# A 32-row block form of the chunk inverses in a two-layer decoder's recurrence, with an earlier state load and a new step order

## The chip, the cores and the metric

The kernel runs on one core of a Trainium2 chip. The metric is the device time of one launch in microseconds (us). The time before is the median of three runs.

## What is computed

One inference step of a two-layer decoder for 256 prompt tokens and 8 samples of 8 tokens (320 tokens, width 2048). Layer A mixes tokens with the RWKV-7 recurrence over 32 heads of size 64; layer B is stick-breaking attention over a paged cache of 2048 keys per sample. The change touches the recurrence alone:

```python
def step(S, inp):
    r_t, w_t, k_t, v_t, kk_t, a_t = inp
    sa = jnp.einsum("bhvk,bhk->bhv", S, -kk_t)
    S = (S * w_t[:, :, None, :] + sa[..., None] * (kk_t * a_t)[:, :, None, :]
         + v_t[..., None] * k_t[:, :, None, :])
    o_t = jnp.einsum("bhvk,bhk->bhv", S, r_t)
    return S, o_t
```

## The kernel before, in words

The program has three parts in a row: the projections r, k, v, g of layer A; the recurrence; and a trunk with the output projection, layer B's projections and the attention. TensorE runs the projections as three passes (high and low parts) over 320 tokens.

The recurrence treats 16 tiles of 128 channels, two heads each, one head in partitions 0 to 63 and one in 64 to 127 (`halves`). The 256 prompt tokens are four chunks of 64 (NCH = 4), and the 64 sample tokens are a fifth (CH = 5). Inside a chunk the recurrence is a triangular system: its strictly triangular 64x64 matrix has to be inverted. The samples' chunk has 8x8 blocks only. Each tile passes three stages, one slot apart:

- **F** (front) makes decays and the scaled rows AR, BZ and KZ.
- **P** (products) makes the chunk matrices, and from them the inverse X. AB (L1517) and s4 (L1523) multiply BZ and KZ with AR; D keeps the 8x8 diagonal blocks. Their inverse Y comes by doubling: D transposed (Dt), D squared (D2, D2t), its fourth power (D4t), W and Y. The rest of the triangle follows the same way: Yt, E, Et, E2, E2t, E4t, Z1, Z2, X. Each of these fifteen steps is the helper `each` (L1495 to L1499): one 64x64 by 64x64 matmul for each chunk and half, ten where all five chunks take part and eight where four do. A transpose is such a matmul with the identity I2. Vn, Bn and Kn are transposes too and stay. ScalarE or VectorE takes every result out of PSUM (L1220, L1378).
- **R** (run) walks through the chunks: U, SA, S, ST for each of four, and U4, SA4, O4, SN, Q4 for the samples. Q4 (L1618) multiplies the samples' loaded states s0t; SN (L1649) multiplies 32-row pieces. Then O0 to O3, mean, cen, csq, var, lnv, rstd, on, ong, oy, y, xh and xl normalise the outputs and split them for the next projection. SA0 takes the X of its tile.

In slot n, F works on tile n, P on tile n - 1 and R on tile n - 2; there are 18 slots. The order in which each engine issues the steps of a slot is written out in ORDER (L328 to L337): a step such as R.t.SA0 is stage, engine (t TensorE, v VectorE, a ScalarE, g GpSimd) and name. `side_by_side` merges the three stages by their place in it. All engines are in order; between them the steps wait on semaphores through `Marks`. PSUM banks go round in TensorE's order of steps, four for P and three for R (`Banks`). Slot 0 also runs the last group of projection g, slot 17 most of the first group of wo.

SyncE loads the inputs of the tiles. Within a slot it waits for the steps that free s, k, r, a and v (the last is freed by TensorE's Vn), loads them, and then loads the samples' states s0t of tile n - 1 (L1071 to L1076).

Of the kernel before, what the change touches and what calls it, by code (L numbers as in the profile page):

```python
# [18 lines left out]
ALU = mybir.AluOpType  # L19
# [10 lines left out]
L = 64  # L30
NCH = SEQ // L
# [297 lines left out]
F.a.sq F.a.ka1 R.t.U0 R.a.Q4 R.a.SA4 R.t.Q4 R.a.O0 P.t.AB R.t.SA0 R.g.Vnx R.v.U0 F.v.cs R.t.U4 P.t.s4 R.t.S0  # L329
F.a.kk0 R.v.SA0 R.t.SA4 R.a.SP1 R.t.O0 R.a.O4 F.t.ss R.t.U1 R.v.U4 P.a.Dt R.t.O4 P.t.Dt R.t.SA1 P.v.D R.t.SN  # L330
F.a.Pc P.a.D2t R.a.SP2 R.v.ST0 P.v.D4s P.a.D2 P.a.D4t R.t.S1 P.t.D2t P.t.D2 R.g.SAx F.a.ln F.g.k2 R.t.U2
R.a.O2 P.v.FR R.a.O1 F.a.rn F.a.Pi P.t.W R.t.SA2 R.a.O3 R.v.U1 P.v.KK F.a.Pm R.v.SA1 P.t.D4t R.t.S2 R.t.O2
P.v.s3 R.v.SNa R.v.ST1 F.g.csm R.v.U2 F.v.ssm R.a.SP3 R.v.SA2 P.g.ID P.a.Yt P.a.Vn R.t.O1 R.a.csq P.v.W
P.a.Et P.a.E R.t.U3 R.v.ST2 R.v.U3 P.t.Y R.t.SA3 P.t.Vn R.t.O3 R.a.lnv R.a.rstd P.t.Yt R.t.mean P.a.E2t
F.t.bon P.t.Et P.t.E R.v.SA3 P.v.Y R.t.var F.g.Rz F.g.ka P.t.Z1 P.a.E2 P.t.E2t F.v.rk R.v.cen F.v.kk P.t.E2
F.v.Az R.a.ong P.a.Bn P.a.E4t R.a.xh P.t.Bn F.v.Bz F.v.bonus P.v.Z1 P.t.Z2 P.t.E4t R.v.on P.v.Z2 P.t.Kn
R.t.S3 R.v.ST3 P.a.Kn F.g.Kz P.v.X P.t.X R.g.SNb R.g.oy R.g.y R.v.xl""".split()  # L337
# [50 lines left out]
def products_of_chunk(c_, pe, q, m, k, half=None, banks=None):  # L388
# [11 lines left out]
READ_BY = {"AB": ("v", "D", "FR", "KK"), "s4": ("v", "D4s", "s3"), "Vn": ("a", "Vn"), "Bn": ("a", "Bn"),  # L400
# [50 lines left out]
def make_masks(c_, pool):

    masks, blk, blkm, I2, m8, mFI, mSI, m3, keep, mJ = (
        c_.masks, c_.blk, c_.blkm, c_.I2, c_.m8, c_.mFI, c_.mSI, c_.m3, c_.keep, c_.mJ)
# [31 lines left out]
    for m in (m8, mFI, mSI, m3):  # L486
# [9 lines left out]
    made(pool.tensor_copy(mFI[:, 1], mSI[:, 1]))  # L496
    made(pool.tensor_tensor(mFI[:, 0], mSI[:, 0], m8[:], ALU.subtract))
# [455 lines left out]
def recurrence(nc, c_, a):  # L953

    with ExitStack() as ctx:
# [19 lines left out]
        D, Dt, D2, D2t, D4t, W = (sb(x, [P, CH, L]) for x in ("D", "Dt", "D2", "D2t", "D4t", "W"))  # L975
        Yt, E, Et = (sb(x, [P, NCH, L]) for x in ("Yt", "E", "Et"))
        FR, KK = ([sb(f"{x}{j}", [P, NCH, 2, L]) for j in range(2)] for x in ("FR", "KK"))
        S3 = [sb(f"S3{j}", [P, 3, L]) for j in range(2)]
        Y, X, Vn, Bn, Kn = ([sb(f"{x}{j}", [P, CH, L]) for j in range(2)] for x in ("Y", "X", "Vn", "Bn", "Kn"))
# [13 lines left out]
        gate_exp, gate_ln = sem("gate_exp"), sem("gate_ln")  # L993
        g_stored = 16 * 16 + 1
# [24 lines left out]
        def _(sp):  # L1019
# [25 lines left out]
            for slot in range(TILES + 2):  # L1045
# [120 lines left out]
        def _(act):  # L1166
# [1683 lines left out]
```

## Time and profile before

| | us |
|---|---|
| median of 3 runs | 2034.37 (2025.7 to 2036.75) |
| profiled execution, its own time | 2030.11 |
| its span | 2028.4 |
| TensorE matmuls busy in the span | 1886.5 (93%) |
| VectorE, ScalarE, GpSimd busy | 1014.0, 815.6, 244.3 |
| slots 2 to 16 of the recurrence | 338.0, from 540.2 to 878.2 |

The window that begins at 522.9 us is slot 1 from its AB on, the one at 540.2 us slots 2 to 16, the one at 810.0 us one slot of these. A slot is taken from the first matmul of Q4 to the next tile's. In the trace each fp32 matmul leaves two records, so a step of ten matmuls shows as x20. A record's duration is from its start to its modelled end, and records overlap: how long a step holds TensorE is read from its start to the start of what follows. VectorE, ScalarE and GpSimd instructions likewise overlap a little. "issue" is time for which the profile shows nothing that was waited for.

### The profile page before, as it was taken

What the parts mean: (1) busy time and instruction counts of PE and PEld (TensorE: products, weight loads), DVE (VectorE), ACT (ScalarE), POOL (GpSimd) and SP (SyncE); (2) the same over time, 40 slices, a digit from 0 to 9 for tenths busy, and PEclk for the clock granted to TensorE, in tenths of its full rate; (3) what the DMA queues carried; (4) which work ended last, traced back from release to release, by engine and by line L of the source; (5) the groups of instructions that cost most, each with busy time, mean ns of one, the idle gap of its engine ahead of it and who ended that gap; (6) DMA issues with size and microseconds to landing.
All of it is one profiled execution on the core that took longest, in us unless ns stands there. A gap on an engine that the chain in (4) does not pass through costs nothing.

```text
span 2028.4 us, 49604 instructions
## 1 busy us (share of the span) xinstructions
PE 1886.5 (93%) x20798; PEld 1623.7 (80%) x20798; DVE 1014.0 (50%) x1686; ACT 815.6 (40%) x1443; POOL 244.3 (12%) x308
## 2 busy tenths in 40 slices
PE   7999999999999999999999899999999999777797
PEld 7988999999888888879998677677777677343697
DVE  7744363634455556634544543443455444677344
ACT  4234232334455555523333333332333444655233
POOL 0200000000244444413200000000000000110032
PEclk9999999999999999989999999999999999999899
DMA  7545555544132322105488999999999999999541
GB/s 284 173 143 177 165 181 171 170 158 149 56 106 85 91 89 84 55 22 189 150 333 315 411 414 419 397 425 424 425 424 424 407 422 383 415 407 378 230 145 73
DMA packets 122959, 505.55 MB, mean 249 GB/s; under 512 B 16033, under 2 KB 55330, under 8 KB 77474
## 3 DMA queue, kind: packets, MB, share of 16 engines
q1 hardware_dynamic: 122754, 502.60, 64.9%
q8 instruction: 155, 2.54, 0.5%
q14 instruction: 50, 0.41, 0.1%
HBM read 470.24 MB, written 32.32 MB: 248 GB/s over the span
## 4 chain that ended last, share of the span: by engine, by line
PE 31%; DMA 16%; DVE 3%; ACT 2%; issue 2%; SPq 1%; DVEq 0%; ACTq 0%
DMA at_vraw<-in_cache_v 16%; PE psP L2566 8%; PE psP L2568 7%; PE psP L2567 7%; PE at_psO L2616 5%; PE at_psS L2595 3%; SPq L1979 1%; PE psP L2661 0%; PE at_psT L2607 0%; DVE wlo L2328 0%; SPq L2019 0%; DVE at_o_new L2483 0%; ACT at_p_w L2286 0%; ACT at_p_w L2284 0%; SPq L1997 0%
## 5 line engine op out<-in xcount | busy, mean ns | idle before, releaser
L2566 PE MATMUL psP<-xhi,whi 128*128 128x320 f32 x1488 | 477.6, 321 | 2.5 <-DVE xlo L2453 1.9
L2567 PE MATMUL psP<-xlo,whi 128*128 128x320 f32 x1488 | 462.3, 311 | 0.0
L2568 PE MATMUL psP<-xhi,wlo 128*128 128x320 f32 x1488 | 462.2, 311 | 0.0
L2566 PEld LDWEIGHTS psP<-xhi,whi 128*128 128x128 f32 x1488 | 282.0, 189 | 67.1 <-issue 66.4
L2328 DVE TENSOR_TENSOR wlo<-wraw,whi 128x2048 fp32r<-128x2048 f32 x92 | 212.9, 2315 | 209.0 <-ACT whi L2154 208.7
L2154 ACT ACTIVATE whi<-wraw 128x2048 fp32r<-128x2048 f32 x92 | 176.0, 1913 | 279.9 <-PE psP L2568 278.3
L2567 PEld LDWEIGHTS psP<-xlo,whi 128*128 128x128 f32 x1488 | 282.3, 190 | 0.1
L2568 PEld LDWEIGHTS psP<-xhi,wlo 128*128 128x128 f32 x1488 | 281.8, 189 | 0.0
L131 PE MATMUL psP<-xhi,whi 128*128 128x320 f32 x704 | 218.4, 310 | 2.8 <-DVE wlo L166 2.3
L132 PE MATMUL psP<-xlo,whi 128*128 128x320 f32 x704 | 217.8, 309 | 0.0
L133 PE MATMUL psP<-xhi,wlo 128*128 128x320 f32 x704 | 217.8, 309 | 0.0
L2616 PE MATMUL at_psO<-at_vraw,at_st 128*32 128x512 f32 x1000 | 129.2, 636 | 54.9 <-DMA at_vraw<-in_cache_v 45.8
L166 DVE TENSOR_TENSOR wlo<-wraw,whi 128x2048 fp32r<-128x2048 f32 x47 | 107.8, 2293 | 144.7 <-ACT whi L160 144.7
L160 ACT ACTIVATE whi<-wraw 128x2048 fp32r<-128x2048 f32 x47 | 89.8, 1910 | 161.9 <-PE psP L133 161.9
L131 PEld LDWEIGHTS psP<-xhi,whi 128*128 128x128 f32 x704 | 132.2, 188 | 3.9 <-DVE wlo L166 2.9
L132 PEld LDWEIGHTS psP<-xlo,whi 128*128 128x128 f32 x704 | 132.2, 188 | 0.1
L133 PEld LDWEIGHTS psP<-xhi,wlo 128*128 128x128 f32 x704 | 132.2, 188 | 0.0
L2595 PE MATMUL at_psS<-at_kraw,at_qp 128*32 128x256 f32 x2048 | 124.9, 385 | 0.2 <-DMA at_kraw<-in_cache_k 0.2
L2616 PEld LDWEIGHTS at_psO<-at_vraw,at_st 128*32 128x32 f32 x1000 | 27.5, 112 | 109.0 <-DMA at_vraw<-in_cache_v 59.4
L2231 ACT ACTIVATE at_st<-at_psT 128x256 f32<-128x256 f32 x64 | 24.3, 380 | 203.3 <-PE at_psT L2607 203.3
L2595 PEld LDWEIGHTS at_psS<-at_kraw,at_qp 128*32 128x32 f32 x2048 | 60.9, 111 | 46.3 <-issue 13.2
L394 PE MATMUL psP<-xhi,whi 128*128 128x320 f32 x256 | 89.2, 348 | 1.3 <-DVE wlo L166 0.8
(378 smaller groups left out, 3212.9 us busy)
## 6 DMA issues: line engine op xcount, KB each, us to landing
wraw<-in_weights SPq DMA_DIRECT2D x160, 1024.0 KB, 6.1
at_kraw<-in_cache_k SPq DMA_DIRECT2D x96, 1024.0 KB, 11.1
at_vraw<-in_cache_v SPq DMA_DIRECT2D x94, 1024.0 KB, 11.1
at_kraw<-in_cache_k SPq DMA_DIRECT2D x64, 512.0 KB, 9.5
at_vraw<-in_cache_v SPq DMA_DIRECT2D x62, 512.0 KB, 10.6
rw_s0t<-in_s0T SPq DMA_DIRECT2D x16, 256.0 KB, 3.1
o_wkv_s<-rw_SN SPq DMA_DIRECT2D x16, 256.0 KB, 2.3
resT<-in_xT SPq DMA_DIRECT2D x8, 320.0 KB, 5.1
```

The lines of the kernel that those rows point to most:

```text
L131: pe.matmul(out, wh, c_.xhi[:, kc, :], start=(kc == 0), stop=False)
L132: pe.matmul(out, wh, c_.xlo[:, kc, :], start=False, stop=False)
L133: last = pe.matmul(out, wl, c_.xhi[:, kc, :], start=False, stop=(kc == NM - 1))
L160: act.activation(c_.whi[:, q % 2], c_.wraw[:, q], ACT.Copy).then_inc(c_.whi_ready, 1)
L166: dve.tensor_tensor(c_.wlo[:, q % 2], c_.wraw[:, q], c_.whi[:, q % 2], ALU.subtract).then_inc(c_.wlo_ready, 1)
L2154: act.activation(whi[:, i % 2], wraw[:, q], ACT.Copy).then_inc(c_.whi_ready, 1)
L2328: dve.tensor_tensor(wlo[:, i % 2], wraw[:, q], whi[:, i % 2], ALU.subtract).then_inc(c_.wlo_ready, 1)
L2566: pe.matmul(out, wh, c_.xhi[:, kc, :], start=(kc == 0), stop=False)
L2567: pe.matmul(out, wh, c_.xlo[:, kc, :], start=False, stop=False)
L2568: last = pe.matmul(out, wl, c_.xhi[:, kc, :], start=False, stop=(kc == NM - 1))
L2595: last = pe.matmul(psS[32 * j:32 * j + 32, 0:BK].rearrange("p (t s) -> p t s", t=KB), qp[:, b % 2, j, 32 * i:32 * i + 32], keys, start=(i ...
L2616: last = pe.matmul(psO[32 * g:32 * g + 32, :], st[:, k % 2, pg, 32 * g:32 * g + 32], values_of(k, pg, g), start=(k % NBLK == 0 and pg == 0 ...
```

## The change

The inverses are made for 32x32 diagonal blocks of the 64x64 triangles instead of whole. The buffers D to Y hold such blocks in compact form, [128, 5, 32]: partitions 0 to 31 the first block of head 0, 32 to 63 its second, and so on, so a chunk needs four matmuls of 32x32 by 32x32 (`by_fourths`), one in each quarter of the partitions. AA computes the diagonal blocks from BZ and AR directly (64 rows, 32 stationary columns, 32 moving). The steps D2, W, D4t and Y run over five chunks, E, Z1, E2t and X over four. The transposes Dt, D2t, Yt, Et and X1t are done by VectorE, 32x32 at a time. E2, E4t, Z2 and the transposing or second-copy matmuls Dt, D2t, Yt and Et leave TensorE: inside 32 rows there are four 8x8 blocks, and E to the power four is zero. The off-diagonal 32x32 corner of X follows from the two diagonal inverses and the corner A12 of the product AB, by two steps of eight matmuls each (Ht, XB), of 64 stationary and 32 moving columns. Y4 (GpSimd) spreads the samples' compact blocks into X, and Xa (ScalarE) the first diagonal block. s4 no longer computes the samples' product that AA now gives. FR shrinks to the half that R reads; F (VectorE) masks the part of AA that E needs.

The load of s0t moves to the head of SyncE's slot. ORDER is new. In the last slot the pieces of the wo split hang on rstd and on instead of SP3 and cen. GpSimd makes the additional masks before the recurrence. The waits that free BZ and KZ name the last of their readers.

```diff
--- before.py
+++ after.py
+R.t.Q4 R.t.U0 P.t.AB R.a.Q4 F.a.sq P.t.AA R.v.U0 R.t.U4 P.v.D R.t.SA0 P.t.Kn R.v.U4 P.g.ID R.v.SA0 P.v.KK R.t.S0
+R.g.Vnx R.t.SA4 F.t.ss R.v.ST0 R.a.SA4 P.v.FR F.a.ka1 R.g.SAx R.t.U1 P.v.Dt P.a.A12 R.t.O4 R.v.U1 R.t.SA1 R.a.O4
+P.t.D2 R.v.SA1 F.v.cs R.t.S1 P.a.D2 R.a.SP1 R.t.SN P.v.D2t F.g.csm R.v.ST1 P.v.F R.a.SP2 P.a.Kn R.t.U2 R.v.SNa F.a.Pc
+F.g.k2 P.t.W F.a.kk0 R.v.U2 P.t.D4t P.v.W R.t.SA2 P.a.D4t R.t.O1 R.v.SA2 F.v.ssm R.t.O0 R.a.O1 R.t.S2 F.a.Pm P.t.Y
+R.v.ST2 F.a.ln R.t.U3 R.a.O0 R.a.SP3 P.t.Vn F.a.Pi R.v.U3 P.v.Y F.a.rn R.t.SA3 R.t.O2 R.v.SA3 P.v.Yt R.t.O3 F.v.rk
+R.a.O2 P.t.E R.a.O3 F.v.kk R.t.S3 P.a.E R.t.mean P.a.Vn P.v.Et F.g.ka P.t.E2t R.v.cen P.t.Z1 P.g.Y4 P.a.E2t R.a.csq
+P.t.s4 F.g.Kz P.v.Z1 R.v.ST3 P.t.X R.t.var F.g.Rz P.v.X P.v.s3 F.t.bon P.v.X1t R.a.lnv P.t.Ht R.a.rstd P.t.Bn R.v.on
+P.a.Ht F.v.Bz P.t.XB R.a.ong P.a.Bn F.v.Az R.g.oy P.a.Xa P.a.XB F.v.bonus R.g.y R.g.SNb R.a.xh R.v.xl
...
@@ make_masks @@
-    made(pool.tensor_tensor(mFI[:, 0], mSI[:, 0], m8[:], ALU.subtract))
+    made(pool.memset(c_.side[:], 0.0))
+    for g in range(4):
+        rows, cols = slice(HL * g, HL * g + HL), slice(HL * (g % 2), HL * (g % 2) + HL)
+        made(pool.tensor_copy(c_.mD[rows, :], m8[rows, cols]))
+        made(pool.tensor_copy(c_.mF[rows, :], mSI[rows, 0, cols]))
+        made(pool.tensor_copy(c_.I4[rows, :], c_.ident[rows, rows]))
+        made(pool.memset(c_.side[rows, g % 2:g % 2 + 1], 1.0))
+    made(pool.tensor_tensor(c_.mF[:], c_.mF[:], c_.mD[:], ALU.subtract))
...
@@ recurrence, buffers @@
-        D, Dt, D2, D2t, D4t, W = (sb(x, [P, CH, L]) for x in ("D", "Dt", "D2", "D2t", "D4t", "W"))
-        Yt, E, Et = (sb(x, [P, NCH, L]) for x in ("Yt", "E", "Et"))
+        D, Dt, D2, D2t, D4t, W, Y = (sb(x, [P, CH, HL]) for x in ("D", "Dt", "D2", "D2t", "D4t", "W", "Y"))
+        FI, Yt, E, Et, E2t, Z, XD, XDt = (sb(x, [P, NCH, HL]) for x in ("FI", "Yt", "E", "Et", "E2t", "Z", "XD", "XDt"))
+        A12, Ht = sb("A12", [P, NCH, L]), sb("Ht", [P, NCH, L])
+        FR = [sb(f"FR{j}", [P, NCH, L]) for j in range(2)]
...
@@ sync, at the head of each slot, ahead of the loads of s, k, r, a and v @@
+                if 0 <= t - 1 < TILES:
+
+                    if t >= 3:
+                        R.t.wait(sp, "Q4", t - 3)
+                        R.v.wait(sp, "SNa", t - 3)
+                    sp.dma_start(s0t[(t - 1) % 2][:], a["s0T"][t - 1]).then_inc(s0_in[(t - 1) % 2], 16)
...
@@ gpsimd, products @@
+                    elif name == "Y4":
+                        Q.v.wait(pool, "Y", t)
+                        if t >= 2:
+                            R.t.wait(pool, "SA4", t - 2)
+                        Q.g.done(pool.tensor_tensor(X[t % 2][:, NCH].rearrange("p (i s) -> p i s", i=2),
+                                                    Y[:, NCH].unsqueeze(1).to_broadcast([P, 2, HL]),
+                                                    c_.side[:].unsqueeze(2).to_broadcast([P, 2, HL]), ALU.mult), name)
...
@@ scalar, products @@
+                    if name == "A12":
+                        Q.v.wait(act, "FR", t)
+                        ps = psP[:, banks_p.of("AB")].rearrange("p (c x l) -> p c x l", c=NCH, l=L)[:, :, 0, HL:L]
+                        Q.a.done(act.activation(A12[:, :, HL:L], ps, ACT.Copy, scale=c_.side[:, 0:1]), name)
+                    elif name == "Xa":
+                        Q.v.wait(act, "X", t)
+                        Q.a.done(act.activation(X[t % 2][:, 0:NCH, 0:HL], XD[:], ACT.Copy, scale=c_.side[:, 0:1]), name)
+                    elif name in ("Ht", "XB"):
+                        Q.t.wait(act, name, t)
+                        out = Ht[:, :, 0:HL] if name == "Ht" else X[t % 2][:, 0:NCH, HL:L]
+                        ps = psP[:, banks_p.of(name), 0:NCH * HL].rearrange("p (c l) -> p c l", l=HL)
+                        Q.a.done(act.activation(out, ps, ACT.Copy), name)
...
@@ vector, products @@
+                    elif name == "Dt":
+                        Q.v.wait(dve, "D", t)
+                        Q.v.done(dve.transpose(flat(Dt[:]), flat(D[:])), name)
...
+                        out, base, n = {"W": (W, W, CH), "Y": (Y, W, CH), "Z1": (Z, Y, NCH), "X": (XD, Z, NCH)}[name]
...
@@ tensor, products @@
+                def by_fourths(out, lhs, rhs, n):
 
                     for c in range(n):
+                        for r in fourths:
+                            last = pe.matmul(out[r, c * HL:c * HL + HL], lhs[r, c], rhs[r, c], start=True, stop=True)
+                    return last
+
+                def corner(out, lhs, rhs):
+
+                    for c in range(NCH):
                         for r in halves:
-                            last = pe.matmul(out[r, c * L:c * L + L], lhs[r, c], I2[r, :] if rhs is None else rhs[r, c],
-                                             start=True, stop=True)
+                            last = pe.matmul(out[r, c * HL:c * HL + HL], lhs[r, c], rhs[r, c], start=True, stop=True)
                     return last
...
+                    elif name == "AA":
+                        F.v.wait(pe, "Az", t)
+                        F.v.wait(pe, "Bz", t)
+                        for c in range(CH):
+                            for g, rows in enumerate(fourths):
+                                r, cols = halves[g // 2], slice(HL * (g % 2), HL * (g % 2) + HL)
+                                last = pe.matmul(ps[rows, c * HL:c * HL + HL], BZ[j][r, c, cols], ar[r, c, 0, cols],
+                                                 start=True, stop=True)
...
+                    elif name == "Ht":
+                        Q.a.wait(pe, "A12", t)
+                        Q.v.wait(pe, "X1t", t)
+                        Q.t.done(corner(ps, A12, XDt), name)
+                    elif name == "XB":
+                        Q.a.wait(pe, "Ht", t)
+                        Q.v.wait(pe, "X", t)
+                        Q.t.done(corner(ps, Ht, XD), name)
```

## Rows read from the trace of the kernel before

**Rows 1.** Windows: length; PE, PEld, DVE, ACT, POOL busy (x); clock, DMA share, GB/s.

```profile
522.90:540.20 17.30, 14.60 (x378) 12.95 (x378) 9.10 (x19) 9.11 (x22) 6.21 (x7) 1.00 0.33 103
540.20:878.20 338.00, 320.08 (x8575) 293.39 (x8575) 196.87 (x510) 189.17 (x538) 137.73 (x160) 1.00 0.27 79
810.00:831.00 21.00, 20.77 (x572) 19.25 (x574) 12.67 (x33) 12.14 (x35) 8.34 (x11) 1.00 0.26 76
```

**Rows 2.** Who waited for whom, TensorE, slots 2 to 16: total us, times, longest.

```profile
PE psP L1499 <- issue: 6.0, 8, 1.4
PE rw_psR L1618 <- DMA rw_s0t<-in_s0T: 1.2, 1, 1.2
```

**Rows 3.** Timeline of TensorE in one slot: start, us, instruction group.

```profile
698.11 1.09 PE L1618 MATMUL rw_psR<-rw_AR,rw_s0t 64*64 64x16 f32 x32
699.02 0.45 PE L1517 MATMUL psP<-rw_AR,rw_BZ 64*64 64x128 f32 x4
...
700.80 0.31 PE L1600 MATMUL rw_psR<-rw_U,rw_X 64*64 64x64 f32 x4
...
705.60 0.75 PE L1499 MATMUL psP<-rw_Dt,rw_D 64*64 64x64 f32 x20
706.18 0.75 PE L1499 MATMUL psP<-rw_D,rw_Dt 64*64 64x64 f32 x20
...
713.52 0.66 PE L1499 MATMUL psP<-rw_FR,rw_Yt 64*64 64x64 f32 x16
713.99 0.74 PE L1473 MATMUL rw_psR<-stage_a,rw_blkm 64*64 64x320 f32 x4
714.53 0.66 PE L1499 MATMUL psP<-rw_Y,rw_Et 64*64 64x64 f32 x16
```

**Rows 4.** Timeline of TensorE around SN, the one step of another tile shape.

```profile
704.05 0.31 PE L1600 MATMUL rw_psR<-rw_U,rw_X 64*64 64x64 f32 x4
704.29 0.66 PE L1649 MATMUL rw_psR<-rw_Vnx,rw_Kn 32*64 32x256 f32 x8
704.78 0.61 PE L1649 MATMUL rw_psR<-rw_SAx,rw_Bn 32*64 32x256 f32 x8
705.32 0.33 PE L1600 MATMUL rw_psR<-rw_Vn,rw_Kn 64*64 64x64 f32 x4
705.48 0.28 PE L1600 MATMUL rw_psR<-rw_SA,rw_Bn 64*64 64x64 f32 x4
```

**Rows 5.** Timeline of TensorE in the attention, a step with 32 stationary columns.

```profile
1751.23 0.65 PE L2650 MATMUL psP<-at_kN,at_qn 128*32 128x64 f32 x32
```

**Rows 6.** Groups of TensorE weight loads, whole span: 32 and 64 stationary columns.

```profile
L2595 PEld LDWEIGHTS at_psS<-at_kraw,at_qp 128*32 128x32 f32 x2048 | 60.9, 111 | 46.3 <-issue 13.2 <-DMA at_kraw<-in_cache_k 0.6
L1618 PEld LDWEIGHTS rw_psR<-rw_AR,rw_s0t 64*64 64x64 f32 x512 | 17.0, 135 | 6.4 <-issue 4.6 <-DMA rw_s0t<-in_s0T 1.4 <-ACT xhi L1262 0.4
```

**Rows 7.** Groups of VectorE, slots 2 to 16.

```profile
L1378 DVE TENSOR_TENSOR rw_Y<-psP,rw_W 128x320 f32<-128x320 f32 x15 | 7.2, 481 | 0.0
L1370 DVE TENSOR_TENSOR rw_S<-psP,rw_m 128x192 f32<-128x192 f32 x15 | 5.2, 348 | 0.0
```

**Rows 8.** Timeline of ScalarE, the end of R in the same slot.

```profile
714.76 0.53 ACT L1251 ACTIVATE stage_a<-rw_psR,consts 128x320 f32<-128x320 f32 x1 [0.16 <-PE rw_psR L1473]
...
717.37 0.65 ACT L1258 ACTIVATE stage_a<-stage_a,vec 128x320 f32<-128x320 f32 x1 [0.82 <-DVE stage_a L1415]
...
719.93 0.47 ACT L1262 ACTIVATE xhi<-rw_yv 128x320 fp32r<-128x320 f32 x1 [1.32 <-POOL rw_yv L1161]
```

**Rows 9.** Timeline of VectorE, the end of R in the same slot.

```profile
716.72 0.61 DVE L1415 TENSOR_TENSOR stage_a<-stage_a 128x320 f32<-128x320 f32 x1
...
720.44 0.49 DVE L1418 TENSOR_TENSOR xlo<-rw_yv,xhi 128x320 fp32r<-128x320 f32 x1
720.85 0.22 DVE L1389 COPY rw_U<-rw_psR 128x64 f32<-128x64 f32 x1
```

**Rows 10.** Page, part 2: GB/s in 40 slices of 50.7 us.

```profile
GB/s 284 173 143 177 165 181 171 170 158 149 56 106 85 91 89 84 55 22 189 150 333 315 411 414 419 397 425 424 425 424 424 407 422 383 415 407 378 230 145 73
```

More of the change, by code:

```diff
@@ L328 @@
 ORDER = """
[L329 to L337, printed above, removed]
+R.t.Q4 R.t.U0 P.t.AB R.a.Q4 F.a.sq P.t.AA R.v.U0 R.t.U4 P.v.D R.t.SA0 P.t.Kn R.v.U4 P.g.ID R.v.SA0 P.v.KK R.t.S0
[6 more added lines that the diff above has]
+P.a.Ht F.v.Bz P.t.XB R.a.ong P.a.Bn F.v.Az R.g.oy P.a.Xa P.a.XB F.v.bonus R.g.y R.g.SNb R.a.xh R.v.xl
+""".split()
 AT = {x: k / len(ORDER) for k, x in enumerate(ORDER)}
@@ L1290, in beside @@
                 elif slot == TILES + 1:
-                    for q, step in ((2, "SP3"), (3, "xh")):
+                    for q, step in ((2, "rstd"), (3, "xh")):
                         for k in range(QC):
@@ L1439, in beside @@
                 elif slot == TILES + 1:
-                    for q, step in ((2, "cen"), (3, "xl")):
+                    for q, step in ((2, "on"), (3, "xl")):
                         for k in range(QC):
@@ L1449, in _ @@
             pe.wait_ge(masks, c_.n_masks)
+            pe.wait_ge(corners, 2)
             halves = [slice(64 * h, 64 * h + 64) for h in range(2)]
+            fourths = [slice(HL * g, HL * g + HL) for g in range(4)]
             def free_p(name, t):
@@ L1456, in free_p @@
                     if tile >= 0:
-                        eng, *by = READ_BY[x]
-                        for y in by:
-                            (Q.v if eng == "v" else Q.a).wait(pe, y, tile)
+                        for y in READ_BY[x].split():
+                            (Q.v if y[0] == "v" else Q.a).wait(pe, y[2:], tile)
             def free_r(name, t):
@@ L1465, in free_r @@
                     if tile >= 0:
-                        eng, *by = READ_BY[x]
-                        for y in by:
-                            (R.v if eng == "v" else R.a).wait(pe, y, tile)
+                        for y in READ_BY[x].split():
+                            (R.v if y[0] == "v" else R.a).wait(pe, y[2:], tile)
             def over_channels(out, mat, x):
@@ L1585, in products @@
+                        Q.t.done(by_fourths(ps, E, Et, NCH), name)
+                    elif name == "X":
                         Q.a.wait(pe, "E2t", t)
                         Q.v.wait(pe, "Z1", t)
-                        Q.t.done(each(ps, D2t, W, NCH), name)
-                    elif name == "X":
-                        Q.a.wait(pe, "E4t", t)
-                        Q.v.wait(pe, "Z2", t)
-                        Q.t.done(each(ps, D4t, Dt, NCH), name)
+                        Q.t.done(by_fourths(ps, E2t, Z, NCH), name)
+                    elif name == "Ht":
[6 more added lines that the diff above has]
+                        Q.t.done(corner(ps, Ht, XD), name)
@@ L1669, in run @@
                             if c == 0:
[L1670 removed]
+                                Q.a.wait(pe, Q.a.last("Xa", "XB"), t)
                             R.v.wait(pe, f"U{c}", t)
```

193 lines of the change are left out of this document (99 added, 94 removed), and 4 rows, old and new, of the table READ_BY.

## The prediction

> **What bounds the kernel now.** Begin with the windows over the recurrence [rows 1]. Slots 2 to 16 last 338.0 us, 22.5 us each; TensorE is busy in 320.1 of them, VectorE in 196.9, ScalarE in 189.2, GpSimd in 137.7, and the granted clock is 1.00, the upper level of 2.4 GHz. The cleanest slot lasts 21.0 us with TensorE busy in 20.8. Next the waits of TensorE [rows 2]: in 15 slots the largest is "issue", 6.0 us on the matmuls of P, for which no engine answers; 1.2 us, once, go to the samples' states. So these slots are as long as TensorE's list of work, and a step taken off it shortens them, as long as no chain through the other engines takes over. Slot 1 is different: from its AB to the next Q4 it lasts 17.3 us with TensorE busy in 14.6 [rows 1]. There F and P run alone, and the chain of P sets the time.
>
> What is gained here reaches the end: the memory moves 22 GB/s in the slice where the recurrence closes and about 415 through the attention behind it [rows 10], so the long loads start after the recurrence and shift with it.
>
> **What TensorE's list loses.** The timeline of one slot [rows 3] prices a step of P by the distance of starts. Twenty records (ten matmuls) take 706.18 - 705.60 = 0.58 us, sixteen take 713.99 - 713.52 = 0.47. The fifteen steps of `each` that go are six of twenty (Dt, D2, D2t, W, D4t, Y) and nine of sixteen (Yt, E, Et, E2, E2t, Z1, E4t, Z2, X): 3.5 + 4.2 = 7.7 us a slot, a third of it. s4 gives up a fourth of its four matmuls' columns: 0.1 us.
>
> **What it gets.** AA, D2, W, D4t and Y have 20 matmuls each (40 records), E, Z1, E2t and X 16 (32 records): 328 records of 32 stationary and 32 moving columns. Ht and XB have 16 records each, of 64 stationary columns.
>
> The price of such a record is the main unknown. A 64x64 step takes 29 ns a record [rows 3]. Q4 shows that short rows alone don't lower this: 32 records with 16 moving columns hold TensorE from 698.11 to 699.02, 28 ns each, as much as with 64 columns. What doesn't shrink there is the weight load of 64 columns. The attention's step with 32 stationary and 64 moving columns ends 32 records in 0.65 us; with 0.22 us for the last one itself that is 0.43 over 31 distances, 14 ns a record [rows 5]. Its load lasts 111 ns against 135 for 64 columns [rows 6]: 24 ns less for 32 columns fewer. In the new steps both columns are 32 and all four quarters of the array can be in use. Half of 14 is 7 ns if the moving columns set the 14; 14 stands if something else does; 28 if each record has a fixed price. I take 8 ns, near the halved row, since the new shape halves the columns and the rows of that nearest one: 328 x 8 = 2.6 us a slot, from 2.3 at 7 ns to 4.6 at 14. Ht and XB are priced by Q4's row, 32 x 28 = 0.9 us.
>
> The Trainium skill ("TensorEngine Tiling (Array Packing)", Instruction Overhead) speaks against the change: each matmul carries some 60 cycles, and a small dimension should not be tiled further; "TensorE: Matmul & The Clock Gate" (Back-to-back issue gap) gives about 25 ns for 1 to 64 columns. By that the new records would cost 8.2 us and the change would lose. The trace does not agree for 32 stationary columns: 14 ns [rows 5].
>
> **Changes of tile shape.** SN is the only step of another shape now, and shows what one costs [rows 4]. Four records ahead of it hold 0.12 us elsewhere (705.48 is followed at 705.60 [rows 3]) and 0.24 here; its first eight take 0.49 against 0.43 at 54 ns each, its last eight 0.54; the four behind take 0.16 instead of 0.12. Together 0.12 + 0.06 + 0.11 + 0.04 = 0.33 us for going in and out. The new order has seven more such visits a slot: AA; D2; W with D4t; Y; E; E2t with Z1; X. That is 2.3 us, between 0 (if this switch is free where tiles are short) and 3.5 (0.5 each, if the drain is worse). The Trainium skill (the same tiling page, Key Properties) says that a change of tiling mode drains the engine; the row puts 0.33 us on it.
>
> Sum on TensorE: 2.6 + 0.9 + 2.3 - 7.7 - 0.1 = -2.0 us a slot. The cleanest slot of 21.0 us [rows 1] would be one of 19.0.
>
> **The other engines.** VectorE loses D4s, Z2 and half of FR, and W, Y, Z1 and X shrink. It gains F and five transposes of 128x160 and 128x128. No row shows a transpose; the nearest, 128x192 and 128x320, take 0.35 and 0.48 us [rows 7]. I take 0.3 each, from 0.2 to 0.6 (two passes): 1.5 us more, and about 1.3 less from what goes. At 13.1 of 22.5 us it has room even at 0.6. ScalarE trades six copies for four smaller ones. GpSimd gets Y4 and a smaller ID, with 9.2 us busy. These I cost at nothing: TensorE's 19 us cover them; if the cover went, each would add its own length in P's chain. The new masks lie before the recurrence, on an engine with little to do there.
>
> **Chains.** The end of R is the longest: the second statistics matmul starts at 713.99 [rows 3], lnv 714.76, on 716.72, ong 717.37, xh 719.93, xl 720.44, the U0 copy 720.85 [rows 8, 9]. Cut to its links (0.8 from matmul to lnv, lnv 0.5, rstd like it, on 0.6, ong 0.65, 1.9 between ong's end and xh for oy and y on GpSimd, xh 0.5, xl 0.4, U copy 0.2) it needs 6.1 us from var until SA0 can start. From var on the new order gives TensorE var, bon, Ht, Bn, XB, Q4, U0, AB, AA with its visit, and U4: 0.54 + 0.54 + 0.46 + 0.58 + 0.46 + 0.91 + 0.12 + 1.78 + 0.32 + 0.33 + 0.24 = 6.3 us [rows 3, 4]. It just fits. Between other steps of R (S0 to U1, U1 to SA1) TensorE has next to nothing put in, so it will wait there for a VectorE copy: I add 0.2 us a slot. The waits called issue grow too: 572 records a slot become 668, in a shorter slot; 0.2 more. Net -1.6 us a slot, x 15 = -24 us.
>
> Slot 1: its chain has eleven matmul steps of 0.75 us until the last record ends [rows 3], each with a copy of 0.4 to 0.5 behind it. The new one has more links, but matmul links of about 0.5 and copies and transposes of about 0.3. I take -2 us, between 0 and -4. **The state load**: SyncE issues it now behind waits for bonus and Vn. The move takes it ahead of five loads, and its own two waits (Q4 and SNa of tile t - 3) are long met at the head of a slot, so nothing is delayed behind it. It removes the one wait of 1.2 us [rows 2], ahead of the first Q4; -1. The other slots have their states in time. The last slot: the wo pieces hang later on ScalarE and VectorE and may come out 1.5 us either way; 0.
>
> Sum: -24 - 2 - 1 = -27 us. Against the profiled execution's 2030.1 us this is 2003; the median is 4.3 higher, so I forecast 2007.
>
> **Rivals.**
> 1. *Half the gain is lost to R's loop.* The 6.1 against 6.3 us tips over as soon as AA or the switches cost less than taken, or on, oy or xh come late. What speaks for it: TensorE's new list leaves little slack between R's steps. Against: the named waits are small today [rows 2]. Price 0.8 us x 15 = 12: 2019. Chance 0.16.
> 2. *14 ns a record.* 328 x 6 = +2.0 us a slot: nothing is left but the waits, +6, -3 outside: 2037. It is the nearest measured row itself. Chance 0.13; half within 0.5%, half above.
> 3. *A fixed price per record, slower.* Q4's 28 ns at 16 columns holds for every record: 328 x 20 = +6.6 us, net +5 a slot, +75 us: 2107. It decides against the change above 13 ns a record, in the nine new steps. Against it stands the 14 ns of rows 5. At the skill's 25 ns it would be 2092. Chance 0.06.
> 4. *Switches free.* If short tiles hide the drain, 2.3 x 15 = 35 us more go, bounded by R's loop at about half: 1985. Chance 0.10.
> 5. *Doesn't do what it says*: nothing in the diff points to it; the steps replace each other one for one.
>
> **How the numbers follow.** Main case 0.55, 1995 to 2022. About 0.5% (10 us) is what a measurement of this kernel can tell from no change. Faster by more: the main case, rival 4, and half of rival 1, which ends at 2019 +- 8: 0.73. Same: the rest of rival 1 and half of rival 2: 0.16. Slower: the other half and rival 3: 0.11. The range of 1986 to 2034 leaves out rival 3, half of rival 2 and a part of rival 4.
>
> **What would show it.** A slot of about 20.9 us in place of 22.5; by_fourths steps of 0.32 and 0.26 us; each change of shape 0.3 us in and out; transposes near 0.3 us; no wait of Q4 for s0t. I am wrong if by_fourths steps hold TensorE for 0.56 us or more, or if TensorE waits for R's U and SA copies in most slots.

## The result, and the profile after: slower, where faster was forecast

The changed kernel takes 2069.14 us (median of 4 runs, 2064.63 to 2077.45) beside 2032.57 for the kernel before (now the median of 4 runs): ratio 1.0188, 95% interval 1.0142 to 1.0234. The forecast of 2007 us, its range of 1986 to 2034 and its sign are wrong. The profiled span went from 2028.4 to 2064.8 us, +36.4. The first Q4 starts at 542.0 us instead of 540.2 (+1.8), slots 2 to 16 last 368.8 us instead of 338.0 (+30.8), and the rest of the program takes 3.8 us more. So the loss lies where the gain was forecast.

The windows of the changed kernel, columns as in [rows 1]: slot 1, slots 2 to 16, its shortest slot, two stretches inside a slot, and the last slot with the turn to the trunk:

```profile
522.00:542.00 20.00, 15.15 (x466) 12.44 (x467) 8.05 (x22) 6.22 (x18) 4.95 (x7) 0.72 0.35 103
542.00:910.80 368.80, 315.43 (x10019) 257.68 (x10018) 189.01 (x570) 169.07 (x512) 127.61 (x173) 0.94 0.24 72
667.80:689.80 22.00, 19.46 (x674) 15.82 (x671) 11.56 (x36) 10.60 (x34) 8.53 (x12) 1.00 0.24 73
...
698.50:703.00 4.50, 1.84 (x63) 1.21 (x56) 1.27 (x4) 1.48 (x4) 1.50 (x2) 0.82 0.49 156
702.50:712.10 9.60, 9.28 (x262) 8.07 (x266) 3.50 (x12) 3.57 (x12) 1.89 (x3) 0.53 0.02 4
...
910.80:950.00 39.20, 36.23 (x296) 26.51 (x296) 9.30 (x22) 7.54 (x21) 6.52 (x8) 0.78 0.04 13
```

VectorE, ScalarE and GpSimd are all busy for less time than before, so none of them has become the bound. TensorE is idle for 368.8 - 315.4 = 53.4 us against 338.0 - 320.1 = 17.9 [rows 1], 35.5 more. And the granted clock, 1.00 before, is 0.94 on average. It has two levels, 1.2 and 2.4 GHz, so some 0.06 x 368.8 / 0.5 = 44 us of the stage ran at the lower one. There the same work takes up to twice as long: four records of AB in slot 1 hold TensorE for 0.22 us at the upper level and 0.43 at the lower, but 32 records of a 32x32 step last 0.26 and 0.41 from first start to last. So the lower clock cost at most some 22 us of busy time (an estimate). Without these, the busy time would be 315.4 - 22 = 293 against 320: 27 us less, 1.8 a slot. The shortest slot, at 1.00 throughout, has TensorE busy in 19.46 us where the cleanest slot before had 20.77 [rows 1], 1.3 less. So the list of work did shrink, by 1.3 to 1.8 us a slot where 2.0 were forecast. What ate it is idle time and the clock that falls after it.

The waits of TensorE in slots 2 to 16 (total us, times, longest), the answer to [rows 2]:

```profile
PE psP L1561 <- issue: 24.2, 25, 2.0
PE rw_psR L1663 <- issue: 14.2, 12, 2.7
PE rw_psR L1712 <- issue: 2.9, 2, 2.5
PE psP L1554 <- issue: 2.5, 3, 1.1
...
PE rw_psR L1663 <- ACT stage_a L1272: 0.5, 1, 0.5
```

"issue" grew from 10.3 us in three rows (6.0 of them in [rows 2]) to 48.4 in eight. The largest wait with a name is 0.5 us: the chains of R and P are not what holds TensorE. The wait of Q4 for s0t is gone.

The timeline of TensorE in the shortest slot (start, us, group), the answer to [rows 3]:

```profile
670.70 0.56 PE L1604 MATMUL psP<-rw_AR,rw_BZ 64*32 64x32 f32 x40
...
676.50 0.55 PE L1561 MATMUL psP<-rw_W,rw_D2t 32*32 32x32 f32 x40
677.02 0.26 PE L1561 MATMUL psP<-rw_D2t,rw_D 32*32 32x32 f32 x8
677.75 0.45 PE L1561 MATMUL psP<-rw_D2t,rw_D 32*32 32x32 f32 x32 [0.47 <-issue]
...
680.06 0.55 PE L1554 MATMUL psP<-rw_I,rw_in_v 64*64 64x64 f32 x12
681.69 0.45 PE L1554 MATMUL psP<-rw_I,rw_in_v 64*64 64x64 f32 x8 [1.08 <-issue]
...
684.47 0.45 PE L1561 MATMUL psP<-rw_Et,rw_E 32*32 32x32 f32 x32
684.74 0.31 PE L1561 MATMUL psP<-rw_Y,rw_Et 32*32 32x32 f32 x12
685.91 0.38 PE L1561 MATMUL psP<-rw_Y,rw_Et 32*32 32x32 f32 x20 [0.85 <-issue]
```

Forty records of 32x32 take 0.55 us to the modelled end of the last; with 0.22 for that one itself, (0.55 - 0.22) / 39 = 8.5 ns each (8.5 to 9.3 over the slots). I had taken 8. From W's start to D4t's it is 0.52 us, where I had 0.32 plus a share of a change of shape. But three steps are cut in the middle, one after 8 of 40 records, one after 12 of 20, one after 12 of 32. A wait for data or for a bank stands ahead of a step's first matmul. These cuts are not waits of the program.

Counted over all of TensorE's instructions in the trace (matmuls, weight loads and the sequencer's own, such as semaphore waits), 39 of the 41 gaps of more than 0.45 us in slots 2 to 16 stand 256 instructions or a multiple of it apart, exactly. In the kernel before it is 9 of 14, at the same places of the count. The page's part 3 says what comes in that size. Before and after:

```profile
span 2028.4 us, 49604 instructions
...
q8 instruction: 155, 2.54, 0.5%
```

```profile
span 2064.8 us, 52736 instructions
...
q8 instruction: 167, 2.74, 0.5%
```

3132 instructions more, 3072 of them matmul and weight-load records of TensorE, are 12 packets and 0.20 MB more: 64 bytes each, 256 to a packet of 16 KB. A matmul in fp32 leaves two records, each with a weight load, so it is four instructions, and 64 matmuls empty a packet, whatever their size. Each of the 39 gaps ends 1.2 to 1.6 us after a packet of this queue has landed. That gives the theory tested below: **TensorE has run out of instructions**, because the small matmuls use up the packets faster than these come.

VectorE's new rows in slots 2 to 16, the answer to [rows 7] (us in total, mean ns), with xl behind them:

```profile
L1411 DVE STREAM_TRANSPOSE rw_Dt<-rw_D 128x160 f32<-128x160 f32 x15 | 5.0, 335 | 0.0
...
L1420 DVE STREAM_TRANSPOSE rw_Et<-rw_E 128x128 f32<-128x128 f32 x15 | 4.7, 311 | 12.9 <-ACT rw_E L1251 12.9
...
L1473 DVE TENSOR_TENSOR xlo<-rw_yv,xhi 128x320 fp32r<-128x320 f32 x14 | 11.6, 826 | 27.7 <-ACT xhi L1293 27.7
```

The transposes cost what was taken. xl takes 826 ns where it took 490 [rows 9]: the new order puts GpSimd's SNb beside it.

### The profile page after: what moved, and what is told of

Read it like the earlier page. It is cut to its first block, busy times and chain, and to the rows that moved or that the text cites. A ratio compares the mean times of both kernels' runs of the same rounds, so it can differ in the third digit from the quotient of the medians.

```text
span 2064.8 us, 52736 instructions
## 1 busy us (share of the span) xinstructions
PE 1881.3 (91%) x22334; PEld 1586.4 (77%) x22334; DVE 1008.0 (49%) x1750; ACT 792.7 (38%) x1411; POOL 242.9 (12%) x341
## 4 chain that ended last, share of the span: by engine, by line
PE 30%; DMA 17%; DVE 3%; issue 2%; ACT 1%; SPq 1%; DVEq 0%; ACTq 0%
DMA at_vraw<-in_cache_v 17%; PE psP L2629 7%; PE psP L2631 7%; PE psP L2630 7%; PE at_psO L2679 4%; PE at_psS L2658 3%; SPq L2042 1%; PE psP L2724 0%; PE at_psT L2670 0%; SPq L2082 0%; DVE at_o_new L2546 0%; DVE at_p_rc L2574 0%; DVE at_w L2479 0%; ACT at_p_w L2349 0%; ACT at_p_w L2347 0%
## 5 line engine op out<-in xcount | busy, mean ns | idle before, releaser
L2658 PEld LDWEIGHTS at_psS<-at_kraw,at_qp 128*32 128x32 f32 x2048 | 61.6, 112 | 48.4 <-issue 16.9
```

The lines of the kernel that those rows point to most:

```text
L2658: last = pe.matmul(psS[32 * j:32 * j + 32, 0:BK].rearrange("p (t s) -> p t s", t=KB), qp[:, b % 2, j, 32 * i:32 * i + 32], keys, start=(i ...
```

## Experiments

Theory A: the supply of TensorE's instructions binds; records cost by their number. Theory B: array time and the order of steps bind; records cost by their columns.

**1. The state load alone** (the kernel before, with only SyncE's load of s0t moved to the head of the slot).

```diff
@@ sync @@
+                    sp.dma_start(s0t[(t - 1) % 2][:], a["s0T"][t - 1]).then_inc(s0_in[(t - 1) % 2], 16)
...
-                    sp.dma_start(s0t[(t - 1) % 2][:], a["s0T"][t - 1]).then_inc(s0_in[(t - 1) % 2], 16)
```

> Kernel before with only the load of the samples' states moved to the head of each slot. Both theories: the one wait of 1.2 us for s0t ahead of the first Q4 goes, nothing else; 0 to -2 us.

2027.51 us beside 2032.67: ratio 0.9982, interval 0.9959 to 1.0004. The move does no harm here; a gain can't be told from none.

**2. The same work in more matmuls** (the kernel before, with AB and s4 in pieces of 64 columns and the four sums over channels in five pieces each; s4's lines are not shown).

```diff
-                    last = pe.matmul(out[r], mat[r, r], x[r], start=True, stop=True)
+                for k in range(5):
+                    kk_ = slice(L * k, L * k + L)
+                    for r in halves:
+                        last = pe.matmul(out[r, kk_], mat[r, r], x[r, kk_], start=True, stop=True)
...
-                                    last = pe.matmul(out[r, cc], lhs[r, c], flat(ar[r, c]),
+                                for i in range(2):
+                                    cc = slice(2 * L * c + L * i, 2 * L * c + L * i + L)
+                                    for r in halves:
+                                        last = pe.matmul(out[r, cc], lhs[r, c], ar[r, c, i],
```

> Kernel before, same sums in the same order and tile shape, but AB and s4 in pieces of 64 columns and the four sums over channels (ss, bon, mean, var) in five pieces of 64: 676 matmul records a slot for 572, about as many as the changed kernel's 668, and about 0.3 us more of array time. Theory A (TensorE's instructions arrive in pieces of 256 and not faster than one piece in some 4.3 us; the changed kernel is bound by their number): slots of 24 to 24.5 us, waits called issue of 2 us or more a slot, +22 to +30 us. Theory B (the loss is made by the changes of tile shape, or by the new order): slots of 22.8 us, +3 to +6 us.

2060.14 us beside 2032.67, ratio 1.013 (1.0086 to 1.0173), +27: A's figure, and far outside B's. Its slots 2 to 16, in the window and the two largest waits of TensorE:

```profile
540.50:908.10 367.60, 335.24 (x10112) 316.01 (x10108) 198.54 (x513) 192.24 (x540) 137.91 (x160) 0.98 0.25 73
```

```profile
PE psP L1501 <- issue: 11.8, 18, 3.1
PE rw_psR L1641 <- issue: 5.5, 2, 2.8
```

No 32x32 tile and no new change of shape is in it, the order is the old one, and the same stops come up, 18 of its 22 gaps of more than 0.45 us at packet boundaries, with the clock at 0.98 behind them. Of the 29.6 us that its slots are longer, 14.4 are idle time of TensorE (32.4 against 17.9) and 15.2 busy time. Of the latter the lower clock is at most some 7 (estimate as above) and the pieces some 5 (0.58 us for a sum in five pieces against 0.54, 0.23 for eight records of AB against 0.22). Its "issue" is 25.6 us, 1.7 a slot, against 10.3 before; A had 2 or more.

**3. Half the small matmuls** (the changed kernel; `by_fourths` issues quarters 1 and 3 only, and what is made of the results is multiplied by zero, so the inverses take no part in the output).

```diff
-                        for r in fourths:
+                        for r in fourths[0:4:2]:
```

> Changed kernel with by_fourths computing only the first and third quarter of the partitions, and the inverses' results multiplied by zero on their way to X: 144 of 668 records a slot left out, all changes of tile shape, the new order and every other step left as they are. Theory A (instruction supply): the waits called issue fall to those of the kernel before, slots of 19.5 to 21 us, -50 to -75 us against the changed kernel, so about 2000 us. Theory B (tile shapes or order): only the array time of the records goes, 144 x 8 ns = 1.2 us a slot, -18 us, so about 2050 us.

2012.57 us, ratio 0.9903 to the kernel before (0.9867 to 0.9939), 57 below the changed one.

```profile
541.30:857.00 315.70, 294.31 (x7859) 241.26 (x7857) 188.17 (x570) 168.24 (x512) 127.48 (x173) 0.97 0.28 83
```

The order, the shapes and their changes, and all other engines' work are those of the changed kernel, and slots take 21.05 us instead of 24.6. I had priced the 144 records that went at 144 x 8.5 ns = 1.2 us of array time a slot. Even that is too much, for with two quarters the records start twice as far apart:

```profile
611.29 0.50 PE L1561 MATMUL psP<-rw_D,rw_Dt 32*32 32x32 f32 x20
620.59 0.44 PE L1561 MATMUL psP<-rw_Et,rw_E 32*32 32x32 f32 x16
```

That is (0.50 - 0.22) / 19 = 15 ns a record. The same steps of 40 and 32 records take 0.55 and 0.45 us in the changed kernel. So half the records give back about 0.25 us a slot as array time (an estimate from these rows) and 3.5 in the measured slot, 25 ns each. This speaks against the order and the switches of shape as the cause. "Issue" fell from 48.4 to 16.8 us, not quite to the 10.3 of the kernel before as A had it, and the time is 2012.57 where A had about 2000; the difference from the changed kernel is inside A's 50 to 75.

**4. Wide blocks, few instructions** (the changed kernel's algebra and VectorE transposes, but in 64-wide buffers with 64x64 matmuls, without AA; 484 records a slot).

```diff
-                        for r in fourths:
-                            last = pe.matmul(out[r, c * HL:c * HL + HL], lhs[r, c], rhs[r, c], start=True, stop=True)
+                        for r in halves:
+                            last = pe.matmul(out[r, c * L:c * L + L], lhs[r, c], rhs[r, c], start=True, stop=True)
```

> The changed kernel's algebra (32x32 diagonal inverses, VectorE transposes, corner by Ht and XB, state load first) but in buffers 64 wide and matmuls of 64x64 by 64: no AA, no 32-row tile shapes, and 484 records a slot. The order is the changed one with D4s, s4, s3 and F moved. Theory A: neither instruction supply nor list binds at more than 19.5 to 20.5 us a slot; -30 to -45 us against the kernel before, about 1990 us. Theory B with the order at fault: slots stay at 23 us or more, 2035 us or more; with tile shapes at fault: as A, so that this run alone does not part these two.

2029.07 us, ratio 0.9993 (0.9972 to 1.0013): 40 us better than the changed kernel, though each small step costs the array more (20 records of 64x64 hold it for 0.58 us), but far from the 1990 expected.

```profile
PE rw_psR L1635 <- DVE rw_ST L1436: 11.1, 14, 0.8
PE psP L1542 <- DVE rw_W L1415: 9.1, 15, 0.6
PE rw_psR L1635 <- DVE rw_U L1425: 7.1, 16, 0.9
...
PE rw_psR L1635 <- issue: 1.7, 3, 0.9
```

"issue" has all but gone (3.1 us in all), and copies have taken its place: 31 us of waits with a name. Instructions are no longer short; steps of R and P wait behind others on VectorE. I had left that term out. The time alone would not part the two theories, since B with the order at fault had 2035 or more; the rows do.

**5. A burst by itself** (the kernel before; ahead of the first tile's sum of squares TensorE multiplies masks into a spare bank, which is no part of the function).

```diff
+                        if t == 0:
+                            for k in range(1024):
+                                q = slice(32 * (k % 4), 32 * (k % 4) + 32)
+                                pe.matmul(psF[q, 0:32], blk[q, q], sq[q, 0:32], start=True, stop=True)
+                            for w in (64, 128):
+                                for k in range(1024):
+                                    h = halves[k % 2]
+                                    pe.matmul(psF[h, 0:w], blk[h, h], sq[h, 0:w], start=True, stop=True)
```

> The kernel before with three bursts of matmuls of masks into a spare bank (they are not part of the function), ahead of the first tile's sum of squares, where TensorE has nothing else to do: 1024 of 32x32 with 32 columns over the four quarters, then 1024 of 64x64 with 64 columns over the two halves, then 1024 of those with 128 columns. Each has a weight load, so 256 instructions are 128 records. Theory A (TensorE's instructions arrive in 16 KB pieces of 256, none sooner than some 3.3 to 4.7 us after the one before): the first burst takes 8 x 3.3 to 4.7 = 26 to 38 us, that is 26 to 37 ns a record and not the 8.5 ns of the rows, with a gap every 128 records; the second about 29 us (28 ns a record by its rows, hardly held up), the third over 50 us with no gaps. Theory B (the pace of the rows is what a record costs and the gaps have another cause, such as the other engines or the queues at work in the slots): the first burst takes 1024 x 8.5 ns = 9 us. The whole kernel: A about +115 us, B about +95.

I had counted 1024 matmuls as 1024 records; they are 2048, so every length doubles: A expects 52 to 76 us for the first burst, B 17. It took 55, and the whole kernel 2261.51 us (a single run) beside 2027.26, +234 (A 230, B 190). The timeline of TensorE in it:

```profile
503.10 1.93 PE L1486 MATMUL rw_psF<-rw_sq,rw_blk 32*32 32x32 f32 x128 [2.33 <-issue]
506.56 1.93 PE L1486 MATMUL rw_psF<-rw_sq,rw_blk 32*32 32x32 f32 x128 [1.54 <-issue]
510.03 1.93 PE L1486 MATMUL rw_psF<-rw_sq,rw_blk 32*32 32x32 f32 x128 [1.53 <-issue]
513.76 1.93 PE L1486 MATMUL rw_psF<-rw_sq,rw_blk 32*32 32x32 f32 x128 [1.81 <-issue]
517.23 1.93 PE L1486 MATMUL rw_psF<-rw_sq,rw_blk 32*32 32x32 f32 x128 [1.53 <-issue]
```

Groups of exactly 128 records (256 instructions) with nothing between, every 3.47 or 3.74 us. VectorE is busy for 0.25 us in this window and GpSimd for 1.7, so no other engine is behind it. The q8 packets of the same stretch:

```
packet starts (took)   500.49 (1.18)  504.20 (0.96)  507.69 (0.96)  511.16 (1.33)  514.80 (0.96)
TensorE resumes        503.10         506.56         510.03         513.76         517.23
```

Work resumes 1.3 to 1.5 us after a packet has landed, and the next packet starts 1.0 to 1.2 us after work has resumed: 1.0 + 1.4 + 1.1 = 3.5 us a packet, 27 to 29 ns a record. The windows of the three bursts:

```profile
499.00:549.90 50.90, 26.64 (x1803) 24.77 (x1806) 0.25 (x1) 0.47 (x1) 1.68 (x2) 0.51 0.04 11
560.00:610.00 50.00, 50.00 (x1722) 50.00 (x1719) 0.00 (x0) 0.00 (x0) 0.00 (x0) 1.00 0.02 4
630.00:700.00 70.00, 70.00 (x1286) 70.00 (x1284) 0.00 (x0) 0.00 (x0) 0.00 (x0) 1.00 0.01 2
```

With 64 columns a record takes 29 ns, 3.7 us a packet, and the gaps are gone: that size is just fed. With 128 it takes 54 ns. The first burst runs at a granted clock of 0.51, the lower level, though its list is nothing but matmuls. B's 17 us were for the upper level; at the 1.93 us that 128 records take here, sixteen groups are 31 us, and the other 24 of the 55 are the stops.

The Trainium skill ("TensorE: Matmul & The Clock Gate", Part 1, "Wait — 56ns, not 53.3ns?") gives some 25 ns as the least distance of starts however few the columns. As an average over a long row of small matmuls this run agrees (27 to 29 ns); inside a packet it does not (8.5 ns at 2.4 GHz in the rows above).

**6. A smaller dose** (of experiment 2 only the sums over channels).

> The kernel before with only the four sums over channels of a slot in five pieces each: 604 matmuls a slot in place of 572, the same columns. Theory A (supply of instructions) : between the 22.5 us a slot of 572 and the 24.5 of 676, in proportion +0.6 us a slot, so +9 us, ratio about 0.996. Theory B (array time alone): +32 x 3 ns a slot, below +2 us.

Two slips of mine in this text: the kernel has 636 records a slot and not 604 (again two to a matmul), so A's share of experiment 2 is 2.0 x 64 / 104 = 1.2 us a slot, +18 us; and the ratio belonging to +9 us is 1.004. Measured: 2041.67 beside 2027.26, ratio 1.0072 (1.0045 to 1.0098), +14; B's +2 is outside. Its slots are 14.1 us longer, 5.1 of them idle time and 9.0 busy time, of which the pieces explain some 2.5 (0.04 us a sum) and the lower clock at most some 3.5; so this dose parts the theories less sharply than the first.

```profile
541.40:893.50 352.10, 329.09 (x9513) 310.90 (x9508) 197.66 (x513) 192.22 (x541) 137.79 (x160) 0.99 0.25 76
```

**7, 9. The wide kernel with its order mended by hand**, first with many moves, then with the three shown (the copies of U2 and ST3 moved along with them).

```diff
@@ ORDER, the second of the two @@
-P.v.FR F.a.ka1 R.g.SAx R.t.U1 P.v.F P.a.A12 R.t.O4 R.v.U1 R.t.SA1
+P.v.FR F.a.ka1 R.g.SAx R.t.U1 R.v.U1 P.v.F P.a.A12 R.t.O4 R.t.SA1
...
-R.t.SN P.v.D2t F.v.cs F.g.csm R.v.ST1
+R.v.ST1 R.t.SN P.v.D2t F.v.cs F.g.csm
...
-F.v.kk R.t.S3 P.a.E
+F.v.kk P.a.E
-P.t.Z1 P.a.E2t
+P.t.Z1 R.t.S3 P.a.E2t
```

> The kernel with inverses in 64-wide buffers and VectorE transposes (484 matmuls a slot), with its order mended by hand where VectorE's steps held up the state's chain: U1's copy ahead of F and FR, ST1 ahead of D2t and cs, S3 between Z1 and X, and GpSimd's SNb moved away from xl. Theory A (supply of instructions was the bound; at 484 it no longer is, and what is left are waits for copies that stood in the wrong place, 18 us of them in the run before): slots of 20.5 to 21.2 us in place of 22.1, 2008 to 2017 us, faster than both kernels. Theory B (the chain of dependent steps is the bound at 22 us whatever the order): 2026 to 2032.

> The 64-wide kernel with VectorE transposes (484 matmuls a slot) once more, from the order of its first run and not from the second, which had put F and FR so late that A12's copy held D2 by 1.2 us a slot. Three moves only: U1's copy ahead of F, ST1 ahead of D2t and cs with U2 ahead of SNa, and S3 between Z1 and X on TensorE. They aim at its rows' idle time before R's copies (ST 0.8, U 0.4 us a slot) and before X (0.6). Theory A (instructions are no longer short at 484 a slot, what is left are copies in the wrong place): 1.0 to 1.8 us a slot of 22.1, so 2002 to 2015 us, faster than both kernels. Theory B (what is taken out in one place comes back behind the next copy): 2022 to 2032, the same as before.

The first order missed: 2048.82 us, ratio 1.011 (1.0058 to 1.0163). I had moved F and FR back, A12's copy waits for both, and D2 for A12's copy; 11.5 us more are waits for SN's copy on VectorE (L1443). The largest:

```profile
PE psP L1542 <- ACT rw_A L1232: 18.7, 15, 1.2
```

The second gives 2024.07 beside 2030.70: ratio 0.9972 (0.9954 to 0.999). Of the kernels here that compute the whole output it is the only one that is ahead of the kernel before beyond its interval, by 6 us. Its slots 2 to 16:

```profile
542.60:870.80 328.20, 300.97 (x7259) 256.20 (x7257) 208.94 (x585) 172.29 (x496) 128.03 (x158) 0.99 0.26 79
```

```profile
PE psP L1542 <- ACT rw_A L1232: 7.6, 15, 0.5
PE psP L1542 <- DVE rw_W L1415: 5.6, 15, 0.4
```

A's figures fell short both times. The first time is outside B's range too; the second lies in it (2022 to 2032), and much of what B says happened: what is taken out in one place comes back behind the next copy. The waits of 11.1 us for ST L1436 went as meant, but 7.6 us came back as waits for A12. What is left is 301 us of TensorE's list and 27 of idle time, most of it in front of copies.

**8. SNb moved** (the changed kernel; GpSimd's SNb behind k2, away from xl).

```diff
-F.g.k2 P.t.W
+F.g.k2 R.g.SNb P.t.W
...
-R.g.y R.g.SNb R.a.xh R.v.xl
+R.g.y R.a.xh R.v.xl
```

> The changed kernel with one step moved in its order: GpSimd's SNb stands behind k2, early in the slot, and no longer beside VectorE's xl, whose rows went from 493 to 826 ns. If the changed kernel's loss lay in its order around the slot's end, 0.3 us a slot come back: -5 us. Theory A (supply of TensorE's instructions): xl gets its 0.3 us back and the time stays within 3 us, since the slot is bound by instructions.

xl is back at 492 ns, and the kernel takes 2069.03 us, as the changed one did (2069.14). The slower xl was real and cost nothing that these runs show; with four runs of each, spread over 7 and 13 us, a few us either way can't be told.

```profile
L1473 DVE TENSOR_TENSOR xlo<-rw_yv,xhi 128x320 fp32r<-128x320 f32 x14 | 6.9, 492 | 27.4 <-ACT xhi L1293 27.4
```

The runs by the records of a slot (slots 2 to 16; 1, 7 and 8 keep the count of the kernel that each is made from):

| kernel | records | us a slot | largest wait of TensorE |
|---|---|---|---|
| 4, wide | 484 | 22.1 | VectorE's copies |
| 9, wide, order mended | 484 | 21.9 | ScalarE's and VectorE's copies |
| 3, half the small ones | 524 | 21.05 | issue |
| before | 572 | 22.5 | issue |
| 6, channels in pieces | 636 | 23.5 | issue |
| changed | 668 | 24.6 | issue |
| 2, AB in pieces too | 676 | 24.5 | issue |

Of the gaps of more than 0.45 us, those at a packet boundary are 13 of 15 in experiment 3, 18 of 22 in 2 and 43 of 45 in 8, but 2 of 36 in 4 and none of 19 in 9, the kernels with 484 records.

## Why the prediction was wrong, step by step

- *TensorE's list bounds the slots, R's waits are small*: right for the kernel before. R's waits stayed small after (0.5 us the largest named wait), but the list no longer bounds the slots: TensorE is idle in 53.4 of 368.8 us. Rival 1 did not happen.
- *8 ns a record*: right as array time, 8.5. Rival 2 (14 ns) did not happen either.
- *0.33 us a change of shape*: no run takes it out by itself. W and D4t, a visit of two steps, hold TensorE for 0.52 and 0.47 us to the start of what follows, where 2 x 0.32 + 0.33 = 0.97 were taken; all nine small steps together for 4.0 us a slot, where 2.6 + 2.3 were taken. What they cost the steps beside them is not in that. The list as a whole shrank by 1.3 to 1.8 us a slot against 2.0 forecast. Rival 4 did not happen.
- *Transposes 0.3 us, other engines at nothing*: right, 0.30 to 0.34. That xl would grow by 0.33 us was missed, without effect (experiment 8).
- *Slot 1 -2*: wrong. Its AB starts at 522.74 us (522.90 before) and the first Q4 1.8 us later than before, so it is 2.0 us longer. Its window shows the clock at 0.72, where [rows 1] has 1.00, and one "issue" wait of 1.6 us; how much of the miss each of them is was not tried.
- *State load -1*: the wait went; its size is below what experiment 1 can tell.
- *Last slot 0*: it and the rest came out +3.8. The window from the last slot on has the clock at 0.78. The same stretch before has 0.83, so the lower clock there is not new; TensorE is idle for 3.0 us in it after and 1.1 before. This was not followed up.

```profile
878.20:917.40 39.20, 38.08 (x320) 29.56 (x320) 9.24 (x24) 9.19 (x23) 3.43 (x4) 0.83 0.19 69
```

- *The clock*: the prediction reads 1.00 and has no term for a change of it. It cost 1.0 to 1.5 us a slot (315.4 us busy less 320.1 is 0.3 a slot, where the list alone gives 1.3 to 1.8).
- ***"The waits called issue grow too: 572 records a slot become 668, in a shorter slot; 0.2 more."*** This step failed. I had the right rows: 6.0 us of "issue" was the largest wait [rows 2] while TensorE was busy in 320 of 338 us. I took it for noise that grows in proportion. It is the edge of a supply of 256 instructions in 3.5 us or more. The wide steps used 40 matmul records (80 instructions with their loads) in 1.16 us; the new ones use the same 80 in about 0.35, or 0.5 with the change of shape. "Issue" grew by 38.1 us in 15 slots, 2.5 a slot where I had 0.2, and TensorE's idle time as a whole by 35.5, 2.4 a slot. With 2.4 for idle time in place of both 0.2s, the forecast's -2.0 for the list and at most 1.5 for the clock, the sum is +1.9 a slot; measured are +2.05. This is bookkeeping on one trace; what shows the cause are experiments 2, 3 and 5.

Neither of the two signs of being wrong that the prediction names came up: by_fourths steps that are not cut hold TensorE for 0.27 to 0.54 us (medians at the upper clock), below its 0.56, and R's copies are not waited for. The loss came in the row that it had priced at 0.2. Two slips in its figures changed nothing: half of rival 4's 35 us gives 1990 and not 1985, and its chances add to 0.145 for "same" and 0.125 for "slower" where it has 0.16 and 0.11.

Rival 3 had the sign and nearly the size right (28 ns a record, 2107 us; measured 2069) for a reason that is only half right. A record does not hold the array for 28 ns, but a long row of them gets through at 27 to 29 ns each. I had rejected it by the 14 ns of [rows 5]. That row is 32 records long, 64 instructions, a quarter of a packet; a row so short can't show what a row of packets costs.

In slots the packets come every 4.5 us on average (at least 3.3), slower than the 3.5 to 3.7 of the burst (before: 4.8), and the longest stops last 2.0 to 2.7 us where most of the burst's last 1.5 to 1.8. The trace shows what is particular about the three longest. The stop of 2.66 us ends at 701.99; its packet started only at 699.58 us, 4.95 us after TensorE had passed the last packet boundary (694.63); half of all packets in these slots start within 1.8 us of one. In that time the load of a 1024 KB piece of wo is under way, which SyncE issues in slots 4, 6, 8 and 10, with the s0t load right behind it:

```profile
693.99 0.46 SPq L1048 DMA_DIRECT2D wraw<-in_weights  x1
694.54 0.38 SPq L1067 DMA_DIRECT2D rw_s0t<-in_s0T  x1
```

```profile
694.60:699.60 5.00, 4.68 (x130) 3.40 (x126) 4.10 (x13) 2.70 (x9) 2.98 (x5) 1.00 0.90 296
```

The stops that end at 650.3 and 752.4 us (2.5 and 2.0) have the same behind them. The four longest of experiment 2 (2.6 to 3.0 us, at 595, 645, 696 and 744) each follow a wo load, too, with 6.4 to 7.1 us from packet to packet. So heavy traffic goes with late packets. That it makes them late is argued from these coincidences; no run leaves the loads out.

Left open: the share of the clock can't be taken apart from the stops, since it falls behind them. Nor was it tried why a packet starts no sooner than it does.

## What to carry to other kernels

Count instructions, not only columns: divide TensorE's list by 256 instructions (64 fp32 matmuls) and ask of each stretch whether it uses up 256 in less than about 3.5 us. In three places beside the load of wo the packets came only every 6.9 to 7.2 us. In fp32 a long row of 64x64 matmuls with 64 columns was just fed; a long row of shorter ones bought only stops, and then a lower clock. The small size by itself is not the fault: experiment 3 has 32x32 steps too, with 524 records a slot, and the shortest slots of all, though it leaves out half of the small work. Where "issue" is TensorE's largest wait and steps are cut in their middle, take matmuls away before columns. And a pace read from a short row does not hold for a long one.

## What the runs showed that I had not expected

- TensorE's instructions come in packets of 16 KB, 64 bytes an instruction. The burst resumed 1.3 to 1.5 us after a landing, and the next packet started 1.0 to 1.2 us later. In the slots the stops ended 1.2 to 1.6 us after a landing.
- The granted clock falls after such stops and in rows of small matmuls: 0.51 through 50.9 us of 32x32 ones, 1.00 through the 64x64 ones behind them; in the changed kernel 0.53 from 702.5 to 712.1 us, after a stop of 2.66 us, while TensorE was busy in 9.28 of 9.60.
- SNb on GpSimd beside xl on VectorE: 826 against 492 ns for the same instruction.
